# Expert rows gathered for two experts at once, gates moved to the addition of outputs, one eviction ahead of a branch, six probability buffers

## The chip, the cores and the metric

The kernel runs on 1 of the 8 cores of one Trainium2 chip. The metric is the device time of one execution in microseconds. Below, PE is TensorE, DVE is VectorE, ACT is ScalarE, POOL is GpSimd and SP is SyncE, whose queue issues the weight loads.

## The reference, cut to what matters

Twelve stages run on 256 tokens of width 1024 in float32. In order: a gated mixer, a dense feed-forward block, a second mixer, a **mixture of experts**, a dense block, an **attention stage "ab"** (16 heads of 64), a memory attention (4 heads of 256), two dense blocks, an **attention stage "c"** (16 heads with a neighbourhood bias), a memory attention, a dense block. The parts that the change touches:

```python
def moe_swiglu(x, w_router, e_gate, e_up, e_down):        # 8 experts, d_ff 3584
    logits = (t @ w_router).astype(jnp.float32)
    top_val, top_idx = lax.top_k(logits, TOP_K)           # TOP_K = 2
    top_w = jax.nn.softmax(top_val, axis=-1)
    gates = jnp.sum(jax.nn.one_hot(top_idx, N_EXPERTS) * top_w[..., None], axis=1)
    for e in range(N_EXPERTS):
        out = out + gates[:, e:e + 1] * swiglu(t, e_gate[e], e_up[e], e_down[e])
# attention, per head: p = softmax(q k^T * scale + bias) ; o = p v
```

## The kernel before, in words

**Engines and order.** Every engine has its program written out by hand, and engines meet at semaphores. A step such as `("xe", e, half)` is a count on the semaphore of the engine that makes it. The whole program is unrolled; the one branch is described below.

**Weights.** A ring of nine 2 MB slots is filled by SP. In the expert stage each slot is used as two halves of 1 MB, 18 in all, and a load waits until PE has released its half ("used"). In the other stages ACT copies each block to a rounded high part (L525) and DVE subtracts to get the low part (L533). PE then makes three products (L558 to L560).

**Experts.** The tokens of an expert are gathered into 96 slots, `expert_in` ("xe"). For each expert, `pe_gather` multiplies the 256 token rows (`copied`, the stationary operand, 128x128 blocks) by a 0/1 matrix `pick` (96 columns): 8 blocks of width times 2 blocks of tokens, 16 matmul calls, each of which is two records in the trace because the operands are float32. Then 4 more calls (8 records, 1 column each) gather the expert's gates for its slots into bank 7, and DVE copies them to `slot_gate`. The hidden width of 3584 is worked in 7 chunks (`NQ`) of 512. Chunk q of expert e, with c its number in the expert, runs on PE as: `pe_pair_up` (L1081), at c = 1 the scatter of the expert before, `pe_pair_down` of the chunk before (L1128), `pe_four_up` (L1095), `pe_four_down` (L1149), a transpose `pe_expert_turn` (L1113), at c = 1 a transpose of `pick`, and at c = 4 `pe_gather` of the next expert (L1057, then the gates, L1067). ACT applies silu and DVE multiplies silu, gate and up-projection (L2121, L2128). The scatter multiplies the output by `pick` transposed, and DVE adds the result to the token rows (L2089).

**Router and branch.** Before the experts, `dve_router` ranks the logits, gives each token its slot, makes `pick` for expert 0, then the gates, then a flag that says whether some expert has more than 96 tokens. `experts_again` lets PE gather for expert 0 and then makes every engine wait for the flag, load it to a register (L2444) and branch (L136). The body of the branch, a second pass over 16 half-experts, isn't run for these inputs. After the branch ACT evicts the gathered rows of expert 0 (`act_expert_rows`) and PE starts `pe_pair_up(0)`.

**Attention.** The 16 heads go in pairs. For pair j, PE makes the scores (L877), DVE adds the bias and takes the maximum (L1862), ACT takes the exponential (L1356), DVE normalizes (L1877), PE transposes (L890), ACT evicts the transpose (L1366) and PE weighs the values (L906). A head's probabilities lie in one of 4 buffers, so DVE's bias step of head i waits until head i-4 is transposed. PE's order in turn j is scores of pair j+1, weighing of pair j-2, transposes of pair j-1. DVE's order is bias of pair j, normalizing of pair j-1, low part of the output of pair j-3. In "c", POOL prepares each head's bias (L2287, L2289), and DVE subtracts the low parts of eight weight blocks (numbers 4 to 11) before its first bias step.

Of the kernel before, what the change touches and what calls it, by code (L numbers as in the profile page):

```python
# [5 lines left out]
P = 128  # L6
# [36 lines left out]
IN_ORDER = slice(PAIR, PAIR + SLOTS)  # L43
# [7 lines left out]
PAIRS = [(i, i + 1) for i in range(0, C_HEADS, 2)]  # L51
SINGLES = [(i,) for i in range(MEM_HEADS)]
# [5 lines left out]
def build_constants():  # L58
# [27 lines left out]
    low, high = np.arange(PAIR), np.arange(PAIR, SLOTS)  # L86
    add("slot_number", np.tile(np.concatenate([low, low, high, high, high, high]), (P, 1)))
# [51 lines left out]
class Program:  # L139
# [33 lines left out]
    def place_memory(self):  # L173
# [31 lines left out]
        self.slot_gate = put("slot_gate", [P, 2, 2])  # L205
# [27 lines left out]
        at[0] += 4096  # L233
# [8 lines left out]
        self.pick = over("pick", [P, TT, 2 * P], F32, small_at)  # L242
# [6 lines left out]
        def overlay(items):  # L249
# [33 lines left out]
            ("p3", [P, TT, T], F32, None),  # L283
# [6 lines left out]
            ("p3", [P, TT, T], F32, None), ("pT0", [P, TT, T], F32, None), ("pT1", [P, TT, T], F32, None),  # L290
# [6 lines left out]
        self.bank = [nc.alloc_psum_tensor(f"bank{i}", [P, 512], F32) for i in range(8)]  # L297

# [583 lines left out]
def pe_turn_p(p, st, prob, item):  # L882
    pe, nc = p.pe, p.nc
    for i in item:
# [3 lines left out]
        for qt in range(TT):  # L888
            for kt in range(TT):
                mm = nc.tensor.transpose(p.bank[6 + i % 2][:, kt * T + qt * P:kt * T + (qt + 1) * P],  # L890
                                         prob[i % 4][:, qt, kt * P:(kt + 1) * P], p.const("identity"))
# [46 lines left out]
def pe_ab(p, st):  # L938
# [27 lines left out]
    pe_attention(p, st, ab_heads(p, st), PAIRS, [g[f"p{i}"] for i in range(4)], [g["pT0"], g["pT1"]],  # L966
# [5 lines left out]
def pe_c(p, st):  # L972
# [23 lines left out]
    pe_attention(p, st, c_heads(p, st), PAIRS, [g[f"p{i}"] for i in range(4)], [g["pT0"], g["pT1"]], meanwhile)  # L996
# [3 lines left out]
def pe_mem(p, st):  # L1000
# [16 lines left out]
    pe_attention(p, st, mem_heads(p, st), SINGLES, [g[f"p{i}"] for i in range(4)], [g["pT0"], g["pT1"]], meanwhile)  # L1017
# [30 lines left out]
def pe_gather(p, e, new_gates=False):  # L1048
# [1533 lines left out]
```

## Time and profile before

| what | value |
|---|---|
| median of 3 runs | 2691.82 us (2688.63 to 2692.26) |
| profiled execution | 2692.51 us |
| its span, first to last instruction | 2691.3 us |
| PE busy | 2575.4 us (96%) |
| DVE, ACT, POOL busy | 1056.7, 817.7, 176.1 us |
| mean granted PE clock | 0.981 |
| read from HBM | 637.68 MB, 237 GB/s over the span |

The profile is of one execution. Ends of matmuls are modelled, so the distance between starts is what counts for PE. Idle time is put down to what ended it.

### The profile page before, as it was taken

To read this page: it belongs to the slowest core of one execution; us is meant where nothing else is said; L and a number is where in the kernel's file an instruction comes from. 1 tells how busy PE (TensorE), PEld (TensorE's weight loads), DVE (VectorE), ACT (ScalarE), POOL (GpSimd) and SP (SyncE) were. 2 spreads that over 40 slices of the span, in tenths; PEclk is the share of its full clock that TensorE was granted. 3 is DMA by queue.
4 is the path that set the end of the run, shared out by engine and by line. 5 is a ranking of instruction groups with operands and counts; after the bars stand their busy time and mean duration, and the time that the engine had idled before them with its cause. 6 is when DMAs were issued, how large, how long until landed. Compare 5 with 4: busy or idle time off the path is not lost.

```text
span 2691.3 us, 37633 instructions
## 1 busy us (share of the span) xinstructions
PE 2575.4 (96%) x16619; PEld 1747.7 (65%) x16619; DVE 1056.7 (39%) x1458; ACT 817.7 (30%) x1127; POOL 176.1 (7%) x178
## 2 busy tenths in 40 slices
PE   7999998999999999999998998899999998899998
PEld 5788776444444444444447886787887887688886
DVE  4655553010101011010106457736456444655544
ACT  4343342010101001010114435544344433544432
POOL 1200120000000000000000002000000004500000
PEclk9999998999999999999998999999999999899999
DMA  7555447999999999999985544345546547254651
GB/s 246 176 188 188 138 168 290 359 346 368 374 363 374 364 376 363 374 351 362 374 301 172 179 137 141 123 159 202 189 156 204 180 163 201 82 193 152 218 179 57
DMA packets 336507, 641.27 MB, mean 238 GB/s; under 512 B 16084, under 2 KB 128768, under 8 KB 336336
## 3 DMA queue, kind: packets, MB, share of 16 engines
q1 hardware_dynamic: 329840, 618.59, 64.7%
q0 software_dynamic: 6496, 20.20, 2.6%
q8 instruction: 132, 2.16, 0.3%
q14 instruction: 39, 0.32, 0.0%
HBM read 637.68 MB, written 1.05 MB: 237 GB/s over the span
## 4 chain that ended last, share of the span: by engine, by line
PE 89%; DVE 5%; ACT 2%; POOL 2%; DMA 1%; issue 1%; SPq 0%; ACTq 0%; DVEq 0%
PE bank L558 16%; PE bank L559 16%; PE bank L560 16%; PE bank L1081 15%; PE bank L1095 7%; PE bank L1128 7%; PE bank L1149 4%; DVE part_lo L533 2%; PE bank L877 1%; PE bank L1113 1%; PE bank L906 1%; PE bank L1057 1%; PE bank L729 1%; PE bank L570 1%; POOL bias L2153 1%; DMA raw<-in_w_in_dram 1%
## 5 line engine op out<-in xcount | busy, mean ns | idle before, releaser
L533 DVE TENSOR_TENSOR part_lo<-raw,part_hi 128x2048 fp32r<-128x2048 f32 x251 | 576.9, 2305 | 298.7 <-ACT part_hi L525 298.2
L525 ACT ACTIVATE part_hi<-raw 128x2048 fp32r<-128x2048 f32 x251 | 477.3, 1911 | 37.0 <-DMA raw<-in_c_w_in_dram 19.5
L558 PE MATMUL bank<-part_hi,x_hi 128*128 128x512 f32 x1088 | 445.3, 409 | 17.9 <-DVE part_lo L533 14.2
L559 PE MATMUL bank<-part_lo,x_hi 128*128 128x512 f32 x1088 | 438.3, 403 | 0.0
L560 PE MATMUL bank<-part_hi,x_lo 128*128 128x512 f32 x1088 | 432.0, 397 | 0.0
L558 PEld LDWEIGHTS bank<-part_hi,x_hi 128*128 128x128 f32 x1088 | 207.4, 191 | 67.4 <-DVE part_lo L533 20.5
L560 PEld LDWEIGHTS bank<-part_hi,x_lo 128*128 128x128 f32 x1088 | 207.4, 191 | 50.7
L559 PEld LDWEIGHTS bank<-part_lo,x_hi 128*128 128x128 f32 x1088 | 208.0, 191 | 43.8
L1081 PE MATMUL bank<-raw,expert_in 128*64 128x512 f32 x896 | 215.8, 603 | 2.5 <-ACT expert_in L1214 2.5
L1081 PE MATMUL bank<-raw_hi,expert_in 128*64 128x512 f32 x896 | 212.2, 594 | 0.0
L2121 DVE SCALAR_TENSOR_TENSOR h<-silu,slot_gate,bank 128x256 f32<-128x256 f32 x56 | 26.9, 480 | 462.3 <-ACT silu L1565 462.3
L558 PE MATMUL bank<-part_hi,hT_hi 128*128 128x512 f32 x440 | 173.6, 395 | 1.2 <-DVE hT_lo L1599 0.9
L559 PE MATMUL bank<-part_lo,hT_hi 128*128 128x512 f32 x440 | 173.3, 394 | 0.0
L560 PE MATMUL bank<-part_hi,hT_lo 128*128 128x512 f32 x440 | 171.9, 391 | 0.0
L1214 ACT ACTIVATE hT_hi<-bank 128x256 fp32r<-128x256 f32 x110 | 42.1, 383 | 399.0 <-PE bank L729 399.0
L2128 DVE SCALAR_TENSOR_TENSOR h<-silu,slot_gate,bank 128x128 f32<-128x128 f32 x56 | 19.4, 347 | 333.0 <-ACT silu L1571 333.0
L1081 PEld LDWEIGHTS bank<-raw_hi,expert_in 128*64 128x64 f32 x896 | 64.8, 138 | 129.2 <-issue 129.2
L1565 ACT ACTIVATE silu<-bank 128x256 f32<-128x256 f32 x56 | 21.5, 383 | 363.8 <-PE bank L1081 363.8
L1081 PEld LDWEIGHTS bank<-raw,expert_in 128*64 128x64 f32 x896 | 59.7, 137 | 107.4 <-issue 104.7
L1571 ACT ACTIVATE silu<-bank 128x128 f32<-128x128 f32 x56 | 15.5, 277 | 359.6 <-PE bank L1095 359.6
L1599 DVE TENSOR_TENSOR hT_lo<-bank,hT_hi 128x256 fp32r<-128x256 f32 x110 | 46.7, 424 | 196.5 <-ACT hT_hi L1214 196.5
L1095 PE MATMUL bank<-raw,expert_in 128*32 128x256 f32 x1792 | 118.6, 382 | 0.0
(268 smaller groups left out, 3476.4 us busy)
## 6 DMA issues: line engine op xcount, KB each, us to landing
raw<-in_exp_w_gate_dram SPq DMA_DIRECT2D x112, 512.0 KB, 6.6
raw<-in_exp_w_up_dram SPq DMA_DIRECT2D x112, 512.0 KB, 7.5
raw_hi<-in_exp_w_gate_dram SPq DMA_DIRECT2D x112, 512.0 KB, 8.4
raw_hi<-in_exp_w_up_dram SPq DMA_DIRECT2D x112, 512.0 KB, 9.2
raw<-in_exp_w_down_dram SPq DMA_DIRECT2D x56, 1024.0 KB, 12.8
raw_hi<-in_exp_w_down_dram SPq DMA_DIRECT2D x56, 1024.0 KB, 14.1
raw<-in_ffn_w_gate_dram SPq DMA_DIRECT2D x110, 512.0 KB, 4.0
raw<-in_ffn_w_up_dram SPq DMA_DIRECT2D x110, 512.0 KB, 5.2
```

What stands on the lines that cost most here:

```text
L525: p.nc.scalar.activation(p.part_hi[i][:, :], p.raw[i][:, :], ACT.Copy).then_inc(*self.rounded.step((name,)))
L533: p.nc.vector.tensor_tensor(p.part_lo[i][:, :], p.raw[i][:, :], p.part_hi[i][:, :].bitcast(F32), ALU.subtract).then_inc(*self.split.step(( ...
L558: nc.tensor.matmul(out, stat_hi, move_hi, start=start, stop=False, skip_group_check=True)
L559: nc.tensor.matmul(out, stat_hi, move_lo, start=False, stop=False, skip_group_check=True)
L560: return nc.tensor.matmul(out, stat_lo, move_hi, start=False, stop=stop, skip_group_check=True)
L570: mm = nc.tensor.transpose(p.bank[bank][:, k * P:(k + 1) * P], src[:, k * P:(k + 1) * P], p.const("identity"))
L1081: mm = p.nc.tensor.matmul(p.bank[4][half * PAIR:(half + 1) * PAIR, :].rearrange("p (m n) -> p m n", m=2), xe[:, kk, 0:PAIR], w[:, k, :, ha ...
L1095: mm = p.nc.tensor.matmul(p.bank[5][f * FOUR:(f + 1) * FOUR, 0:256].rearrange("p (m n) -> p m n", m=2), xe[:, kk, PAIR:SLOTS], w[:, k, :, ...
L1128: mm = p.nc.tensor.matmul(p.bank[0][half * PAIR:(half + 1) * PAIR, :], p.hT[:, j, d * PAIR:(d + 1) * PAIR], w[:, j, half * 512:(half + 1) ...
L1149: mm = p.nc.tensor.matmul(p.bank[1][f * FOUR:(f + 1) * FOUR, 0:256], p.hT[:, 2, tile * FOUR:(tile + 1) * FOUR], w[:, j, f * 256:(f + 1) * ...
L1214: p.nc.scalar.activation(dst, src, ACT.Copy).then_inc(*p.s.step(key))
L1599: p.nc.vector.tensor_tensor(dst, src, high.bitcast(F32), ALU.subtract).then_inc(*p.v.step(key))
```

## The change

Four edits. (1) Gates are no longer gathered into slots: the 4 one-column matmul calls, the `slot_gate` copy and the waits on both are gone, the hidden product becomes a plain multiplication, and the addition of an expert's output multiplies by the gate of the token row. (2) Experts 1 and 2, 3 and 4, 5 and 6 are gathered together: the same 16 calls with 192 columns, eight of them after chunk 4 and eight after chunk 5 of experts 0, 2 and 4. Expert 7 is gathered alone at chunk 4 of expert 6. There are three `expert_in` buffers for two, and two `pick` buffers of 96 columns for one of 256. (3) The flag is computed before the gates, and ACT evicts expert 0's rows ahead of the branch. (4) Six probability buffers for four; in "c" the low parts of blocks 10 and 11 are made after the first bias step. The constant `slot_number` shrinks from 256 to 96 columns.

```diff
-IN_ORDER = slice(PAIR, PAIR + SLOTS)
+PROB = 6
...
-def pe_gather(p, e, new_gates=False):
+def pe_gather(p, e):
...
-                mm = nc.tensor.matmul(out, p.copied[:, tt, k * P:(k + 1) * P], p.pick[:, tt, IN_ORDER],
+                mm = nc.tensor.matmul(out, p.copied[:, tt, k * P:(k + 1) * P], p.pick(e, tt),
...
-    if new_gates:
-        pe.wait_ge(*p.v.at("gates"))
-    if e:
-        pe.wait_ge(*p.s.at("pickT", e - 1))
-    for j in range(2):
-        for tt in range(TT):
-            mm = nc.tensor.matmul(p.bank[7][:, j:j + 1], p.pick[:, tt, j * P:(j + 1) * P], p.gates[:, tt, e % N_EXP:e % N_EXP + 1],
-                                  start=(j == 0 and tt == 0), stop=(tt == TT - 1), skip_group_check=True)
-    mm.then_inc(*p.t.step(("gate_gathered", e)))
+def gathered_in(e, count):
+    return [i for i in (e + 1, e + 2) if i < count] if e % 2 == 0 else []
...
+def pe_gather_two(p, group, part):
+    pe, nc = p.pe, p.nc
+    first, second = group
+    pe.wait_ge(*p.v.at("pick", second))
+    if part:
+        pe.wait_ge(*p.s.at("xe", second, 0))
+    elif first >= 2:
+        pe.wait_ge(*p.v.at("added", first - 2, 1, 1))
+    for n in range(4):
+        k = part * 4 + n
+        out = p.bank[2 + n // 2][:, (n % 2) * 2 * SLOTS:(n % 2 + 1) * 2 * SLOTS].rearrange("p (i s) -> p i s", i=2)
+        for tt in range(TT):
+            mm = nc.tensor.matmul(out, p.copied[:, tt, k * P:(k + 1) * P], p.picks[:, :, tt * SLOTS:(tt + 1) * SLOTS],
+                                  start=(n % 2 == 0 and tt == 0), stop=(tt == TT - 1), skip_group_check=True)
+    mm.then_inc(*p.t.step(("gathered", first, part)))
...
-        if c == 4 and e + 1 < count:
-            pe_gather(p, e + 1)
+        group = gathered_in(e, count)
+        if c in (4, 5) and len(group) == 2:
+            pe_gather_two(p, group, c - 4)
+        elif c == 4 and group:
+            pe_gather(p, *group)
...
+    p.act.wait_ge(*p.t.at("gathered", group[0], part))        # act_expert_rows, two experts
+    for i, e in enumerate(group):
+        for b in range(2):
+            at = part * 4 + 2 * b
+            made = p.nc.scalar.activation(
+                p.xe[e % 3][:, at:at + 2, :],
+                p.bank[2 + b][:, 0:4 * SLOTS].rearrange("p (k i s) -> p k i s", k=2, i=2)[:, :, i, :], ACT.Copy)
+        made.then_inc(*p.s.step(("xe", e, part)))
...
-            if i >= 4:
-                dve.wait_ge(*p.t.at("p_turned", st, i - 4))
+            if i >= PROB:
+                dve.wait_ge(*p.t.at("p_turned", st, i - PROB))
...
-    p.ring.subtract(*slots[4:12])
+    p.ring.subtract(*slots[4:10])
...
+                  {0: lambda: p.ring.subtract(slots[10], slots[11]), 1: lambda: p.ring.subtract(slots[12]), 3: lambda: p.ring.subtract(slots[13]),
...
-                nc.vector.tensor_tensor(part, part, p.bank[SCATTER_BANK[tt, half]][:, :], ALU.add).then_inc(
-                    *p.v.step(("added", e, half, tt)))
+                nc.vector.scalar_tensor_tensor(out=part, in0=p.bank[SCATTER_BANK[tt, half]][:, :],
+                                               scalar=p.gates[:, tt, e % N_EXP:e % N_EXP + 1], in1=part,
+                                               op0=ALU.mult, op1=ALU.add).then_inc(*p.v.step(("added", e, half, tt)))
...
-        nc.vector.scalar_tensor_tensor(out=p.h[0][:, :], in0=p.silu[0][:, :], scalar=gate[:, 0:1], in1=p.bank[4][:, 256:512],
-                                       op0=ALU.mult, op1=ALU.mult).then_inc(*p.v.step(("pair_h", q)))
+        nc.vector.tensor_tensor(p.h[0][:, :], p.silu[0][:, :], p.bank[4][:, 256:512], ALU.mult).then_inc(
+            *p.v.step(("pair_h", q)))
...
-    pe_gather(p, 0, new_gates=True)
+    pe_gather(p, 0)
+    act_expert_rows(p, [0], 0)
     for q in queues:
         q.wait_ge(*p.v.at("flag"))
```

## Rows read from the trace of the kernel before

**Rows 1.** The page's head: span, and PE's busy time, share and instructions.

```profile
span 2691.3 us, 37633 instructions
...
PE 2575.4 (96%) x16619; PEld 1747.7 (65%) x16619; DVE 1056.7 (39%) x1458; ACT 817.7 (30%) x1127; POOL 176.1 (7%) x178
```

**Rows 2.** Critical chain at chunk 4 of expert 0: start us, us, what.

```profile
530.53 3.55 PE bank L1057 x32
534.08 0.81 PE bank L1067 x8
```

**Rows 3.** Windows: one expert's turn and 10 us of it; busy by engine, PEclk, DMA, GB/s.

```profile
530.53:651.04 120.51, 120.51 (x1082) 52.80 (x1081) 11.79 (x26) 11.67 (x29) 0.00 (x0) 1.00 0.98 366
...
480.00:490.00 10.00, 10.00 (x68) 3.76 (x59) 0.57 (x2) 1.14 (x3) 0.00 (x0) 1.00 1.05 393
```

**Rows 4.** Waits of SP's queue, 450 to 1405 us: total, times, longest.

```profile
SPq L514 <- PE bank L1095: 616.0, 76, 17.4
```

**Rows 5.** Critical chain: matmuls of 128 and of 256 columns, 128x128 weights.

```profile
79.17 2.68 PE bank L808 x24
...
1789.99 3.69 PE bank L877 x16
```

**Rows 6.** Groups by form on DVE: busy, mean ns of one, idle before.

```profile
L1624 DVE SCALAR_TENSOR_TENSOR x_rows<-x_rows,bank 128x512 f32<-128x512 f32 x44 | 28.5, 681 | 21.4 <-PE bank L560 21.4
...
L2089 DVE TENSOR_TENSOR x_rows<-x_rows,bank 128x512 f32<-128x512 f32 x32 | 20.6, 682 | 2.1 <-PE bank L1184 1.5
```

**Rows 7.** PE's own queue: the flag's load and the branch, duration ns and start.

```profile
L2444 PEldq TENSOR_LOAD <-overflow x1: 490/490/490, 446.1 to 446.1; - x1
```

**Rows 8.** The same for the branch instruction of DVE and PE.

```profile
L136 DVEq COMPARE_BRANCH  x1: 72/72/72, 444.0 to 444.0; - x1
L136 PEldq COMPARE_BRANCH  x1: 3825/3825/3825, 446.7 to 446.7; - x1
```

**Rows 9.** Timeline around the branch, PE and ACT.

```profile
441.60 4.62 PE L1057 MATMUL bank<-pick,copied_rows 128*128 128x96 f32 x22 [1.01 <-DVE router_logits L2040]
```

**Rows 10.** The same, after the flag.

```profile
445.84 1.50 PE L1057 MATMUL bank<-pick,copied_rows 128*128 128x96 f32 x12
447.18 0.98 PE L1067 MATMUL bank<-gates,pick 128*128 128x1 f32 x8
...
449.62 0.87 ACT L1214 ACTIVATE expert_in<-bank 128x384 f32<-128x384 f32 x2
...
450.65 3.68 PE L1081 MATMUL bank<-raw,expert_in 128*64 128x512 f32 x8 [2.50 <-ACT expert_in L1214]
```

**Rows 11.** Stage ab, DVE's waits for transposes in all, 1640 to 1720 us.

```profile
DVE p L1862 <- PE bank L890: 5.6, 4, 2.0
```

**Rows 12.** Stage ab, timeline of ACT: two transposed query tiles evicted in turn 2.

```profile
1678.46 0.68 ACT L1214 ACTIVATE qT<-bank 128x256 f32<-128x256 f32 x2
```

**Rows 13.** Stage ab, PE: scores of pairs 4 and 5.

```profile
1678.94 1.13 PE L877 MATMUL bank<-kT,qT 64*128 64x256 f32 x8 [0.88 <-DVE softmax_stats L1874]
...
1683.69 1.13 PE L877 MATMUL bank<-kT,qT 64*128 64x256 f32 x8 [1.13 <-DVE softmax_stats L1874]
```

**Rows 14.** Stage ab, DVE: first bias step of pairs 4 and 6.

```profile
1681.83 0.48 DVE L1862 CUSTOM_DVE_ANT_0 p<-bank,consts,minus_sink 128x256 f32<-128x256 f32 x1 [1.25 <-PE bank L890]
...
1692.17 0.48 DVE L1862 CUSTOM_DVE_ANT_0 p<-bank,consts,minus_sink 128x256 f32<-128x256 f32 x1 [0.85 <-PE bank L890]
```

**Rows 15.** Stage c, timeline: POOL, DVE's subtractions 10 and 11, first bias step.

```profile
2285.17 3.09 POOL L2287 TENSOR_SCALAR bias<-bias 128x384 f32<-128x384 f32 x1
2287.16 5.59 DVE L533 TENSOR_TENSOR part_lo<-raw,part_hi 128x2048 fp32r<-128x2048 f32 x2
...
2292.66 0.41 DVE L1862 CUSTOM_DVE_ANT_1 p<-bank,bias 128x256 f32<-128x256 f32 x1
```

**Rows 16.** Stage c, PE: scores of pairs 0 and 1.

```profile
2285.46 2.08 PE L877 MATMUL bank<-kT,qT 64*128 64x256 f32 x8 [3.17 <-ACT kT L1214]
2294.26 2.08 PE L877 MATMUL bank<-kT,qT 64*128 64x256 f32 x8 [6.73 <-DVE softmax_stats L1862]
```

More of the change, by code:

```diff
@@ L85, in build_constants @@
     add("scan_keep", np.tile((np.arange(2 * T) % GLA_CHUNK != 0).astype(np.float32), (P, 1)))
-    low, high = np.arange(PAIR), np.arange(PAIR, SLOTS)
-    add("slot_number", np.tile(np.concatenate([low, low, high, high, high, high]), (P, 1)))
+    add("slot_number", np.tile(np.arange(SLOTS), (P, 1)))
     e = np.arange(N_EXP)
@@ L232, in place_memory @@
         y0_at = at[0]
-        at[0] += 4096
+        at[0] += 8192
         end = at[0]
@@ L297, in place_memory, with prob, pick @@
         self.bank = [nc.alloc_psum_tensor(f"bank{i}", [P, 512], F32) for i in range(8)]
+    def prob(self, tensors):
+        return [tensors[f"p{i}"] for i in range(PROB)]
+    def pick(self, e, tt):
+        return self.picks[:, (e - 1) % 2, tt * SLOTS:(tt + 1) * SLOTS]
     def const(self, name):
@@ L1352, in act_attention @@
         for i in items[j] if j < m else ():
-            hd, P_ = heads[i], prob[i % 4]
+            hd, P_ = heads[i], prob[i % PROB]
             act.wait_ge(*p.v.at("biased", st, i))
@@ L1522, in act_router, with act_expert_rows @@
         nc.scalar.activation(x, x, ACT.Copy, scale=alpha).then_inc(*p.s.step(("total", n)))
-def act_expert_rows(p, e):
-    if e >= 2:
-        p.act.wait_ge(*p.t.at("four_up", (e - 1) * NQ - 1))
-    for half in range(2):
-        p.act.wait_ge(*p.t.at("gathered", e, half))
-        act_high_and(p, p.xe[e % 2][:, half * 4:half * 4 + 4, :],
-                     p.bank[2 + half][:, 0:4 * SLOTS].rearrange("p (k s) -> p k s", k=4), "xe", e, half)
+def act_expert_rows(p, group, part, into=None):
+    for e in group:
+        if e >= 3:
+            p.act.wait_ge(*p.t.at("four_up", (e - 2) * NQ - 1))
+    if len(group) == 1:
+        for half in range(2):
+            p.act.wait_ge(*p.t.at("gathered", *group, half))
+            act_high_and(p, p.xe[group[0] % 3 if into is None else into][:, half * 4:half * 4 + 4, :],
+                         p.bank[2 + half][:, 0:4 * SLOTS].rearrange("p (k s) -> p k s", k=4), "xe", *group, half)
+        return
+    p.act.wait_ge(*p.t.at("gathered", group[0], part))
[6 more added lines that the diff above has]
+        made.then_inc(*p.s.step(("xe", e, part)))
 def act_experts(p, st, count, ahead=None):
@@ L1584, in act_experts @@
             act_high_and(p, p.pickT[0:SLOTS, :, :], p.bank[7][0:SLOTS, 0:TT * P].rearrange("p (t s) -> p t s", t=TT), "pickT", e)
-        if c == 4 and e + 1 < count:
-            act_expert_rows(p, e + 1)
+        group = gathered_in(e, count)
+        if c == 4 and group or c == 5 and len(group) == 2:
+            act_expert_rows(p, group, c - 4)
     if ahead is not None:
@@ L1862, in dve_attention @@
                 made = nc.vector.tensor_tensor_reduce(
-                    out=rows(prob[i % 4][:, qt, :]), in0=rows(p.bank[4 + i % 2][:, qt * T:(qt + 1) * T]), in1=bias,
+                    out=rows(prob[i % PROB][:, qt, :]), in0=rows(p.bank[4 + i % 2][:, qt * T:(qt + 1) * T]), in1=bias,
                     scale=-scale, scalar=3e38 if hd["sink"] is None else hd["minus_sink"], op0=ALU.add, op1=ALU.min,
@@ L2037, in dve_router @@
     dve_pick(p, 0, 0)
+    nc.vector.tensor_reduce(p.biggest[:, :], out[:, 2 * E:3 * E], AX.X, ALU.max).then_inc(*p.v.step(("biggest",)))
+    dve.wait_ge(*p.v.at("biggest"))
+    nc.vector.tensor_scalar(p.overflow[:, :], p.biggest[:, :], float(SLOTS), None, ALU.is_gt).then_inc(*p.v.step(("flag",)))
     dve.wait_ge(*p.s.at("second_weight"))
@@ L2082, in add @@
             dve.wait_ge(*p.s.at("total", 3))
+            dve.wait_ge(*p.v.at("gates"))
         for tt in halves:
@@ L2127, in dve_experts @@
         dve.wait_ge(*p.s.at("four_silu", q))
-        nc.vector.scalar_tensor_tensor(out=p.h[1][:, 0:P], in0=p.silu[1][:, 0:P], scalar=gate[:, 1:2], in1=p.bank[5][:, P:2 * P],
-                                       op0=ALU.mult, op1=ALU.mult).then_inc(*p.v.step(("four_h", q)))
+        nc.vector.tensor_tensor(p.h[1][:, 0:P], p.silu[1][:, 0:P], p.bank[5][:, P:2 * P], ALU.mult).then_inc(
+            *p.v.step(("four_h", q)))
         if c == 0 and e:
@@ L2132, in dve_experts @@
             y_low(e - 1)
-        if e + 1 < count:
-            if c == 2:
-                dve_pick(p, e + 1, first)
-            if c == 4:
-                dve_slot_gate(p, e + 1)
+        for coming in gathered_in(e, count) if c == 2 else ():
+            dve_pick(p, coming, first)
     if ahead is not None:
```

75 lines of the change are left out of this document (34 added, 41 removed).

## Prediction

> **What bounds the kernel now.** I read the page first: of a span of 2691.3 us PE is busy for 2575.4 [rows 1], so a part counts only if it shortens PE's work or one of PE's waits. I then took the windows and the critical chain through the expert stage. One expert's turn is 120.51 us long with PE busy throughout at a granted clock of 1.00 [rows 3], and the chain there is PE alone, one block behind the other. At chunk 4 it shows the gather as a piece of its own, 3.55 us for 32 records, and the gate gather behind it, 0.81 us for 8 [rows 2]. The DMA share of 0.98 in the same row could make one think of a stage bound by its loads. Two rows speak against it: SP's queue spent 616 us of the stage waiting for PE to free a slot [rows 4], and where loads are outstanding the engines move 393 GB/s against a mean of 366 [rows 3]. So loads follow PE, with 7% to spare. Last I read the timelines around the branch and of both attention stages, where PE does stand idle.
>
> **Part 1 and 2, gathers.** Seven gathers stand in the stage behind the branch (experts 1 to 7). Each costs 3.55 + 0.81 = 4.36 us [rows 2], 30.5 in all. The seven gate gathers (5.7 us) go away altogether. What is left is three gathers for two experts and one for expert 7 alone (3.55). The price of a record with 192 columns isn't in the trace. A record of 1, 96 or 128 columns takes 0.81 / 8 = 0.10, 3.55 / 32 = 0.111 and 2.68 / 24 = 0.112 us [rows 2, 5]: up to 128 columns it costs the same, so something other than the columns sets it, and the 128x128 weights that each record loads are what these have in common. A record of 256 columns takes 3.69 / 16 = 0.231 [rows 5], so there the columns do. In proportion 192 columns take 0.173; allowing a little for a fixed part in it I take 0.17, thus 5.4 us for two experts. The new sum is 3 x 5.4 + 3.55 = 19.8, a **saving of 10.8 us**. The bounds are the two neighbouring prices: 0.111 gives 14.2 in all and a saving of 16.3, 0.231 gives 25.7 and a saving of 4.8.
>
> A rule of the Trainium skill speaks for a cheaper record. "TensorE: Matmul & The Clock Gate", section "Back-to-back issue gap", gives N / 2.4 + 2.5 ns at full clock, 82.5 ns for 192 columns, which is less than the weights' price in [rows 2]; by it the record would stay at 0.111. But it gives 109 ns for 256 columns where [rows 5] show 231, so for these float32 records the trace does not agree, and my sum goes by the row.
>
> Work that goes with it is hidden. DVE's product loses its gate and its addition gains one. A DVE addition of 128x512 from a bank takes 682 ns, and a multiply-and-add of that shape 681 [rows 6]; the gate as a per-row factor I price at the same (a dearer one is covered: DVE is busy for 11.8 of 120.5 us [rows 3], and PE has two blocks to do before it needs the additions). ACT makes eight evictions of 128x192 in place of four of 128x384, under PE's next chunk; it too is busy for 11.7 us. If that cover were gone, the eviction (0.9 us for two of the old ones [rows 10]) would be paid once for each of three groups. The second half of a joint gather waits for the eviction of the first, a whole chunk behind it; PE's later work is queued behind that wait, but it is met some ten us early. The scatter's wait for "xe" is now for a gather of an earlier expert or chunk. SP's loads are moved past nothing; their spacing only shrinks by 1%: 366 GB/s become 366 x 120.5 / 119.1 = 370, against the 393 seen.
>
> **Part 3, the branch.** PE's first product after it starts at 450.65 [rows 10]. ACT's eviction ends at 450.5, but PE's own branch instruction starts at 446.7 and takes 3.83 us [rows 8], so it ends at 450.5 too: moving the eviction ahead removes one of two equal waits. What moves the other is the queue. PE's load of the flag starts at 446.1 [rows 7], when records up to 448.2 are still to run: some nine of the gather and eight of the gates, 17 in the queue. Without the gates' eight, the load is reached eight records earlier. These run at 4.62 / 22 = 0.21 us [rows 9] or, late, at 0.11, so 0.9 to 1.7 us earlier; I take 1.2. PE then leaves its branch at about 449.3, the eviction ends at about 447.9, and ACT's own branch, priced as PE's (0.5 for the flag's load and 3.8), by 452.3. PE's first block gives it work only later: 8 of its 32 records take 3.68 us [rows 10], the other 24 at least half as much each, so the block lasts over 8 us. The flag no longer waits for the gates; nothing waited for it. **1.2 us**, from 0 (a fetch that takes longer because weight loads are still running) to 2.5.
>
> **Part 4, six buffers, stage ab.** DVE waits 5.6 us for transposes, in four waits [rows 11]. All four go, but PE must gain from it. The scores of pair 4 start at 1678.94, directly behind ACT's query tile of 1678.46 + 0.39 [rows 12, 13]: the first two waits are given back there. From pair 5 on PE waits for the bias step: 1.13 us idle before 1683.69 [rows 13], released by DVE, whose steps of pairs 4 and 6 had waited 1.25 and 0.85 [rows 14]. I add these two and a little for the slack they free: **2.3 us**, bounds 0 and 5.6. The memory stages have four heads and never reuse a buffer; nothing there.
>
> **Part 4, stage c.** The first bias step starts at 2292.66, behind the subtractions of blocks 10 and 11, 5.59 us from 2287.16 [rows 15]. PE's scores of pair 0 are done at 2285.46 + 2.08 = 2287.54 [rows 16], so the step can run at 2287.6. PE's scores of pair 1 start 1.6 us behind the step's start (2292.66 to 2294.26), thus at about 2289.2 in place of 2294.26: 5.1 us less idle time of the 6.73 [rows 16]. The two subtractions move behind it; they are late for nobody, since PE reads block 10 only after pair 2's scores. POOL's bias of head 3 is then next in line. POOL and DVE slow each other there (3.09 us for a step [rows 15]), but PE has 36 products queued between the scores of pair 1 and pair 2. Behind that PE is bound by its own work, so I keep the gain. The transposes waited for in c are PE's own order; the two extra buffers bring nothing that I can name. **5.1 us**, from 0 (POOL late) to 7 (also less time at half clock: both scores take 2.08 us for eight records, against 1.13 at the full clock [rows 13]).
>
> **Constants.** 160 columns less are 82 KB ahead of the first weights, at 393 GB/s **0.2 us**.
>
> **The sum** is 10.8 + 1.2 + 2.3 + 5.1 + 0.2 = 19.6. The span becomes 2671.7. The profiled execution took 1.2 us more than its span, and the median shown is 0.7 below it: 2672.2 us. (What cannot be told from no change here is about 0.2%, 5.4 us.)
>
> **The rivals.** (a) *Weights still set the record of 192 columns.* For it: 1 to 128 columns cost the same. Against it: 256 columns cost double. Saving 16.3 in place of 10.8: **2666.7**. This is where the Trainium skill's rule above would lead. Chance 0.12. (b) *The columns cost more, as 256 do.* The moving operand is now in two pieces, 192 floats apart. **2678.2**, chance 0.07. (c) *Stage c gives its gain back*: POOL's bias or a block's landing becomes the wait. For it: one of POOL's two steps for a head takes 3.09 us while DVE subtracts [rows 15]. Against it: PE's 36 products. **2677.3**, chance 0.10. (d) *The attention edits do nothing at all*, PE's idle time only moves: 2672.2 + 7.4 = **2679.6**, chance 0.05. (e) *Loads become the bound*, the slower case. Place: the expert stage, once PE asks for 370 GB/s. If the mean delivered stays at the 366 of now, the 10.8 us are lost, 2683, still faster; it decides against the change when the rate falls below 366: at 355 GB/s an expert takes 124.2 us and the stage 8 x 3.7 = 30 us more, less the 8.8 of the other parts: **2713**. Nothing that lowers the rate is in the diff, and SP waits for PE for 616 us. Chance 0.02 for slower, 0.02 for the 2683 case. The forecast itself has the rest, 0.62.
>
> **How the numbers follow.** The low end takes in (a) with the shorter half-clock stretch, 2666.7 - 1.9, about 2665. The high end takes in (b), (c) and (d), 2680. Together they leave out (e), two of the slow cases at once, and noise of the runs (3.6 us between the three shown), some 0.15. Faster by over 0.2% means below 2686.4: all but (e) and a surprise, 0.96; within 0.2% 0.02; slower 0.02.
>
> **What would show it.** The L1067 group is gone, and the joint gather stands as two pieces of 16 records with 2.7 us each at chunks 4 and 5 of experts 0, 2 and 4; 1.8 says (a), 3.7 says (b). Two turns of experts, a joint gather in one of them, take some 237.7 us in place of 241.0. PE leaves the branch near 449.3. DVE in ab has no wait on L890, and PE starts the output projection 2.3 us sooner after its first scores. In c the gap before the scores of pair 1 is 1.6 us. It is wrong if PE shows new waits for "xe", for a landing, or for POOL's bias, or if the granted clock falls in other places than now.

## The result and the profile after

The changed kernel takes 2661.28 us (median of four runs, 2658.41 to 2662.33) against 2692.04: a ratio of 0.989, with a 95% interval of 0.9877 to 0.9903. It is 30.8 us faster where 19.6 were forecast, and below the forecast's low end of 2665. The profiled execution is the fastest of the four; its span is 2657.2 us. From the head of its page, to be read beside [rows 1]:

```profile
span 2657.2 us, 37338 instructions
...
PE 2553.2 (96%) x16459; PEld 1730.9 (65%) x16459; DVE 1047.0 (39%) x1450; ACT 817.1 (31%) x1138; POOL 178.0 (7%) x178
```

PE is busy for 22.2 us less, and stands idle for 11.9 less.

The critical chain around the branch (start us, us, what). L1065 is the single gather, L1108 the first block of pair 0:

```profile
438.03 6.67 PE bank L1065 x32
444.73 0.50 ACT expert_in L1243
445.23 0.27 issue
445.49 7.09 PE bank L1108 x32
```

the same block in the kernel before:

```profile
450.65 9.69 PE bank L1081 x32
```

and PE's own branch, in the view of that line (duration ns, start us), to be read beside [rows 8]:

```profile
L135 PEldq COMPARE_BRANCH  x1: 3665/3665/3665, 441.7 to 441.7; - x1
```

The eviction ends at 445.2 and PE's branch at 441.7 + 3.67 = 445.3. As in the kernel before, two waits end together. They end sooner, and the block behind them is shorter. Windows of just that block (columns as in [rows 3]) show why, before and after: a granted clock of 0.73 and of 1.00, so in the kernel before a part of it ran at 1.2 GHz.

```profile
450.65:460.34 9.69, 9.69 (x36) 3.13 (x40) 0.00 (x0) 1.14 (x1) 0.00 (x0) 0.73 0.01 2
...
445.49:452.58 7.09, 7.09 (x36) 2.70 (x40) 0.00 (x0) 1.28 (x1) 0.00 (x0) 1.00 0.02 5
```

The chain at the joint gathers behind experts 0 and 2 (L1094), to be read beside [rows 2]:

```profile
522.71 2.60 PE bank L1094 x16
525.31 7.02 PE bank L1108 x32
...
541.55 2.60 PE bank L1094 x16
...
760.18 2.60 PE bank L1094 x16
```

Sixteen records of 192 columns take 2.60 us, 0.163 us each. Two experts' turns take 760.18 - 522.71 = 237.47 us, against twice the 120.51 of [rows 3]. The waits of SP's queue are 605 us for PE's L1122 (the block that [rows 4] have as L1095), so loads still follow PE.

Stage ab as two windows of the same extent, from one POOL step to the same one in the next stage (us, then busy us of PE, PEld, DVE, ACT, POOL, then PEclk, DMA share, GB/s), first the kernel before:

```profile
1610.94:1730.50 119.56, 98.48 (x524) 75.65 (x524) 85.57 (x208) 65.53 (x140) 16.55 (x17) 0.96 0.31 107
```

and the changed one:

```profile
1590.75:1707.54 116.79, 99.65 (x524) 76.12 (x524) 85.52 (x208) 64.97 (x140) 16.53 (x16) 0.94 0.32 109
```

PE's idle time, the window less its busy time, is 17.1 us in place of 21.1. DVE's 5.6 us of waits for transposes [rows 11] are gone from its list.

Stage c, timeline of PE's scores of pairs 0 and 1, to be read beside [rows 16]:

```profile
2258.24 1.14 PE L885 MATMUL bank<-kT,qT 64*128 64x256 f32 x8 [2.22 <-ACT kT L1243]
2261.29 2.08 PE L885 MATMUL bank<-kT,qT 64*128 64x256 f32 x8 [1.91 <-DVE softmax_stats L1902]
```

The gap before the scores of pair 1 is 1.91 us in place of 6.73.

So each part of the change can be seen, near its forecast size or above it, and yet 11 us more are gained. Most of that lies elsewhere. A stage whose instructions are the same in both kernels shows it: the eighth stage, dense, from POOL's step for the first half of the rows to the same step of the next stage. Timeline of POOL, before:

```profile
2028.57 0.56 POOL L2183 TENSOR_TENSOR rstd<-rstd,minus_half 128x1 f32<-128x1 f32 x1 [172.42 <-DVE rstd L1636]
...
2221.79 0.56 POOL L2183 TENSOR_TENSOR rstd<-rstd,minus_half 128x1 f32<-128x1 f32 x1 [172.41 <-DVE rstd L1636]
```

and after:

```profile
2004.75 0.56 POOL L2214 TENSOR_TENSOR rstd<-rstd,minus_half 128x1 f32<-128x1 f32 x1 [171.76 <-DVE rstd L1676]
...
2197.30 0.56 POOL L2214 TENSOR_TENSOR rstd<-rstd,minus_half 128x1 f32<-128x1 f32 x1 [171.76 <-DVE rstd L1676]
```

193.22 us before, 192.55 after, with nothing edited in between. The groups of the lines view (busy us, mean ns of one, idle before) say which records it is, before:

```profile
L558 PE MATMUL bank<-part_hi,x_hi 128*128 128x512 f32 x1088 | 445.3, 409 | 17.9 <-DVE part_lo L533 14.2 <-DVE x_lo L1599 3.7
L559 PE MATMUL bank<-part_lo,x_hi 128*128 128x512 f32 x1088 | 438.3, 403 | 0.0
L560 PE MATMUL bank<-part_hi,x_lo 128*128 128x512 f32 x1088 | 432.0, 397 | 0.0
```

and after:

```profile
L566 PE MATMUL bank<-part_hi,x_hi 128*128 128x512 f32 x1088 | 444.2, 408 | 19.1 <-DVE part_lo L541 15.4 <-DVE x_lo L1639 3.7
L567 PE MATMUL bank<-part_lo,x_hi 128*128 128x512 f32 x1088 | 433.5, 398 | 0.0
L568 PE MATMUL bank<-part_hi,x_lo 128*128 128x512 f32 x1088 | 432.8, 398 | 0.0
```

The middle product of each group of three (the low part of the weights by the high part of the tokens) takes 398 ns in place of 403. These two tables give modelled lengths. Taken from start to start over all 512-column records of a product at the full clock (those with the tokens, and those of the down-projections and output projections), the three are 231.5, 234.4 and 230.3 ns apart before, and 231.2, 231.7 and 231.4 after.

### The profile page after: what moved, and what is told of

Same layout as the page of the kernel before. It is cut to its first block, busy times and chain, and to the rows that moved or that the text cites. A ratio compares the mean times of both kernels' runs of the same rounds, so it can differ in the third digit from the quotient of the medians.

```text
span 2657.2 us, 37338 instructions
## 1 busy us (share of the span) xinstructions
PE 2553.2 (96%) x16459; PEld 1730.9 (65%) x16459; DVE 1047.0 (39%) x1450; ACT 817.1 (31%) x1138; POOL 178.0 (7%) x178
## 4 chain that ended last, share of the span: by engine, by line
PE 89%; DVE 5%; ACT 3%; DMA 2%; issue 1%; POOL 0%; SPq 0%; DVEq 0%
PE bank L566 16%; PE bank L567 16%; PE bank L568 16%; PE bank L1108 15%; PE bank L1122 8%; PE bank L1155 7%; PE bank L1176 4%; DVE part_lo L541 2%; PE bank L885 1%; PE bank L1140 1%; ACT part_hi L533 1%; PE bank L737 1%; PE bank L578 1%; DMA raw<-in_c_w_in_dram 1%; PE bank L914 1%; DMA raw<-in_w_in_dram 1%
## 5 line engine op out<-in xcount | busy, mean ns | idle before, releaser
L2155 DVE TENSOR_TENSOR h<-silu,bank 128x256 f32<-128x256 f32 x56 | 23.6, 421 | 497.2 <-ACT silu L1604 497.2
L1108 PE MATMUL bank<-raw,expert_in 128*64 128x512 f32 x896 | 214.1, 598 | 0.8 <-ACT expert_in L1243 0.8
L1108 PE MATMUL bank<-raw_hi,expert_in 128*64 128x512 f32 x896 | 211.3, 592 | 0.0
L2162 DVE TENSOR_TENSOR h<-silu,bank 128x128 f32<-128x128 f32 x56 | 16.1, 288 | 334.2 <-ACT silu L1610 334.2
L1108 PEld LDWEIGHTS bank<-raw_hi,expert_in 128*64 128x64 f32 x896 | 64.5, 137 | 127.7 <-issue 127.7
L1108 PEld LDWEIGHTS bank<-raw,expert_in 128*64 128x64 f32 x896 | 59.5, 136 | 106.4 <-issue 105.3
L1610 ACT ACTIVATE silu<-bank 128x128 f32<-128x128 f32 x56 | 15.5, 278 | 359.4 <-PE bank L1122 359.4
L1122 PE MATMUL bank<-raw,expert_in 128*32 128x256 f32 x1792 | 118.6, 382 | 0.0
```

Of the source, the lines that this page charges most:

```text
L1108: mm = p.nc.tensor.matmul(p.bank[4][half * PAIR:(half + 1) * PAIR, :].rearrange("p (m n) -> p m n", m=2), xe[:, kk, 0:PAIR], w[:, k, :, ha ...
L1122: mm = p.nc.tensor.matmul(p.bank[5][f * FOUR:(f + 1) * FOUR, 0:256].rearrange("p (m n) -> p m n", m=2), xe[:, kk, PAIR:SLOTS], w[:, k, :, ...
```

## The experiments

"Experts" below is the stretch from POOL's last normalising step ahead of the router to its first behind the experts; "ab" and "c" are the stretches between two such steps around these attentions (c from POOL's first bias step on). "Distance" is the address of the first weight buffer less that of `x_hi`, the token parts, modulo 256 bytes; all weight buffers are 16384 bytes apart and so share it. The table holds all kernels; readings follow one by one.

| kernel | distance | stage 8, us | experts | ab | c | median us | ratio to before, 95% interval |
|---|---|---|---|---|---|---|---|
| before | 96 | 193.22 | 993.4 | 119.6 | 95.7 | 2692.0 | |
| changed | 192 | 192.55 | 977.1 | 116.8 | 89.9 | 2661.3 | 0.9890 (0.9877-0.9903) |
| again | 192 | 192.55 | 977.4 | 121.5 | 89.9 | 2663.95 | 0.9896 (0.9881-0.9911) |
| c_order_back | 192 | 192.5 | 977.5 | 119.6 | 94.1 | 2667.0 | 0.9906 (0.9893-0.9920) |
| four_probs | 192 | 192.6 | 977.6 | 119.8 | 90.4 | 2665.2 | 0.9903 (0.9888-0.9919) |
| same_places | 96 | 193.25 | 979.3 | 119.2 | 91.6 | 2670.3 | 0.9920 (0.9906-0.9933) |
| one_by_one | 192 | 192.6 | 984.4 | 119.6 | 93.1 | 2672.5 | 0.9933 (0.9919-0.9947) |
| branch_back | 192 | 192.6 | 980.9 | 119.7 | 89.9 | 2667.9 | 0.9919 (0.9905-0.9932) |
| before_moved | 192 | 192.55 | 991.7 | 119.9 | 97.8 | 2681.95 | 0.9969 (0.9957-0.9981) |
| moved_320 | 0 | 189.35 | 976.6 | 119.1 | 89.4 | 2647.0 | 0.9840 (0.9827-0.9854) |
| before_32 | 128 | 191.78 | 992.4 | 121.0 | 95.8 | 2675.5 | 0.9948 (0.9935-0.9962) |
| moved_64 | 0 | 189.35 | 979.0 | 118.1 | 90.8 | 2642.4 | 0.9826 (0.9811-0.9841) |
| moved_96 | 32 | 191.78 | 977.3 | 120.0 | 90.1 | 2659.8 | 0.9885 (0.9870-0.9900) |
| moved_448 | 128 | 191.68 | 979.2 | 118.3 | 90.3 | 2653.1 | 0.9860 (0.9845-0.9875) |
| x_apart | 128 | 191.51 | 979.1 | 119.7 | 90.9 | 2657.9 | 0.9876 (0.9861-0.9892) |
| x_with_0 | 0 | 191.12 | 979.1 | 121.0 | 90.5 | 2640.8 | 0.9816 (0.9803-0.9830) |
| x_with_64 | 0 | 189.67 | 977.0 | 119.3 | 89.4 | 2647.9 | 0.9840 (0.9827-0.9854) |
| before_160 | 0 | 189.32 | 993.3 | 119.4 | 94.9 | 2667.25 | 0.9917 (0.9904-0.9931) |

**again**: the changed kernel, no edit.

> The changed kernel itself, once more, to see what one profile of it differs from the next. Theory A (what the first profile gained before the router, 3.4 us in stages whose instructions are the same, comes from where the buffers lie): the same 3.4 us within 0.5, the same spacing of the dense stages' 512-column records (231.6, 232.3, 231.9 ns against 232.2, 235.7, 230.6 before), the same rows of the granted clock at half. Rival B (it was a lucky execution): the gain before the router anywhere between 0 and 3.4 us, and the records' spacing changes from one profile to the next.

Stage 8 and the records repeat to 0.03 us and 0.1 ns. The gain ahead of the router is 1.6 us, not 3.4: here PE was granted half the clock for 3.4 us more near the start. Theory A holds for the records; of the 3.4 us, some 1.8 belong to that one execution. The stages that can be read to a few hundredths are those in which PE never stands still, at full clock. The median is 2663.95, 2.7 us above that of the first comparison, so a difference of some 3 us between two comparisons shows nothing.

**c_order_back**: the subtractions of stage c in their old order.

```
-    p.ring.subtract(*slots[4:10])
+    p.ring.subtract(*slots[4:12])
...
-                  {0: lambda: p.ring.subtract(slots[10], slots[11]), 1: lambda: p.ring.subtract(slots[12]), ...
+                  {1: lambda: p.ring.subtract(slots[12]), ...
```

> The changed kernel with the subtractions of stage c in their old order (all eight weight blocks ahead of the first bias step). The prediction's step: the time of it is lost again, 5.1 us of 2661.3, so 2666.4, and PE stands still 6 to 7 us before the scores of pair 1 instead of 1.9. Rival 1: the biases landed 3 us earlier in the changed kernel's profile and the subtractions now fit before them; then it costs under 2 us. Rival 2: all that stage c gained (8.8 us) hangs on the order, by the subtractions that POOL slowed down: 2670.

Its timeline of PE has

```profile
2262.34 1.32 PE L885 MATMUL bank<-kT,qT 64*128 64x256 f32 x8 [2.77 <-ACT kT L1243]
2271.08 2.08 PE L885 MATMUL bank<-kT,qT 64*128 64x256 f32 x8 [7.43 <-DVE softmax_stats L1902]
```

The gap is back, 7.43 us against 1.91. c takes 94.1 us against 89.9, 4.2 more, and the median rises by 3.1. The step is confirmed, with 4.2 us by the stage and 5.5 by the gap; both rivals fall.

**four_probs**: four buffers used, six kept in memory.

```
-PROB = 6
+PROB = 4
```

> The changed kernel with four probability buffers used instead of six, all buffers where they are. The prediction's step: 2.3 us lost, all of it in stage ab (first bias step of a pair waiting for a turned block of probabilities again), none in stage c and the memory stages: 2663.6. Rival 1: buffers are free in time either way, under 0.5 us. Rival 2: they also carry stage c, where PE would then wait again before the scores of later pairs: 2666 to 2669.

DVE's list of waits in ab has the transposes again:

```profile
DVE p L1902 <- PE bank L898: 6.0, 4, 2.0
```

and the window of the stage reads

```profile
1593.00:1712.80 119.80, 99.76 (x524) 76.55 (x524) 85.44 (x208) 65.55 (x140) 16.55 (x16) 0.94 0.30 106
```

Idle time of PE is 20.0 us again. So the mechanism is right: two buffers more take 3 us of idle time from PE. But `again`, with six buffers, shows what becomes of them:

```profile
1592.82:1714.34 121.52, 104.29 (x524) 79.55 (x524) 85.66 (x208) 65.31 (x140) 16.55 (x17) 0.90 0.30 105
```

It idles for 17.2 us and is busy for 104.3, since its granted clock in the stage is 0.90. Over all the profiles, the five kernels with four buffers (before, before_32, before_moved, before_160, four_probs) idle for 20.0 to 21.2 us in ab and take 119.4 to 121.0, mean 119.9; the thirteen with six idle for 16.9 to 18.4 and take 116.8 to 121.5, mean 119.4. The idle time goes and the stage hardly gets shorter: PE works the same products at a lower mean clock. The clock's own records say so too: in ab PE was granted half the clock for 10.2 to 13.7 us with four buffers (mean 13.0) and for 13.7 to 23.9 with six (mean 18.9). The medians differ by 1.3 us, within the spread. In c four buffers cost 0.5 us. The gain of this part is near 0.5 us, less than the spread of these stages, and not 2.3; that the clock takes the rest back is read from these rows and not tested by itself.

**same_places**: all buffers behind the constants at their old addresses.

```
+        at[0] += 640
         self.params = put("param_rows", [P, P])
...
+        at[0] += 32
         self.overflow = put("overflow", [P, 1], mybir.dt.int32)
```

> The changed kernel with 640 bytes left free behind the constants and 32 behind the routing marks, so that the weight buffers and all behind them lie at the addresses of the kernel before (the change makes the constants 160 columns shorter and drops a small tile). Theory A (placement): the 512-column records of the dense stages go back to a mean of 232.9 ns from 231.9, each of the five dense stages after the first loses 0.66 us, and the stages before the router lose their 3.4 us: 2661.3 + 3.3 + up to 3.4 = 2664.6 to 2668. Rival B (chance, or the change's other parts): within 1 us of the changed kernel, with the records as there.

Stage 8 takes 193.25 us, as in the kernel before; the records are 231.5, 234.4 and 230.5 ns apart, as there:

```profile
L569 PE MATMUL bank<-part_lo,x_hi 128*128 128x512 f32 x1088 | 438.2, 403 | 0.0
```

The median rises by 6.35 us. Theory A holds. Shorter constants (640 bytes) and the dropped `slot_gate` (32) move every weight buffer by 672 bytes, and that alone is worth 6 us of the result. Against the kernel before (2692.31 in this comparison) the change with its places held is worth 22.0 us. Its first block behind the branch is not at the full clock:

```profile
449.72 8.73 PE bank L1110 x32
```

**one_by_one**: a joint record issued as two single ones.

```
+            for i in range(2):
-            mm = nc.tensor.matmul(out, p.copied[:, tt, k * P:(k + 1) * P], p.picks[:, :, tt * SLOTS:(tt + 1) * SLOTS],
+                mm = nc.tensor.matmul(out[:, i, :], p.copied[:, tt, k * P:(k + 1) * P], p.picks[:, i, ...],
```

> The changed kernel with each joint gather record of 192 columns issued as two records of 96, same banks, same places in the program: 96 more records. The prediction's step (a record of 192 columns 0.163 us against 0.111 for one of 96): the two cost 0.222 us, 0.059 us more per pair, 96 pairs: 5.7 us lost, in the three pairs of pieces (16 joint records took 2.60 us; 32 single ones should take 3.55). Rival (the 128-partition weight load isn't what sets a 96-column record and the second record of the same weights is cheaper): under 2 us lost.

Its chain has the pieces at the old price:

```profile
524.55 3.55 PE bank L1095 x32
```

3.55 us against 2.60, six times: 5.7 us, as forecast. The stretch takes 7.0 more; another 1.0 is the first block behind the branch, 8.1 us against 7.09. The granted clock of that block is 1.00 here, so it isn't the clock; what lengthens it is open. The median is 8.6 above that of `again`; the profile has 3.2 us more in stage c too, where nothing was edited.

**branch_back**: first eviction behind the branch, flag behind the gates.

```
     pe_gather(p, 0)
-    act_expert_rows(p, [0], 0)
     for q in queues:
...
+    act_expert_rows(p, [0], 0)
     act_experts(p, moe, N_EXP, lambda: act_ahead(p, moe + 1, 0, 1))
```

(and the two instructions of the flag moved to the end of the router's function).

> The changed kernel with the first eviction behind the branch again and the flag worked out behind the gates. The prediction's step: the branch stretch loses 1.2 to 1.7 us (ACT waits for the flag, takes its branch, loads its table and only then evicts, 1.28 and 0.98 us behind TensorE's own branch of 3.67 us), and the first pair_up stands behind it. Rival 1: TensorE's own branch ends last either way, under 0.5 us. Rival 2: the longer stand of TensorE also brings the granted clock down for the first pair_up (9.69 us before, 7.09 after): 3.5 to 4.5 us lost.

Timeline of ACT and PE behind the branch:

```profile
446.19 1.28 ACT L1243 ACT_TABLE_LOAD   x1 [5.90 <-issue]
447.48 0.87 ACT L1243 ACTIVATE expert_in<-bank 128x384 f32<-128x384 f32 x2
```

```profile
448.03 3.63 PE L1108 MATMUL bank<-raw,expert_in 128*64 128x512 f32 x8 [2.70 <-ACT expert_in L1243]
```

ACT is past its branch instruction (45 ns, at 441.0) but issues nothing until 446.2, then loads its table and evicts; PE's branch is over at 446.0, and PE waits until 448.03. The first block takes 8.78 us and not 7.09, at a granted clock of 0.81. Experts lose 3.5 us, the figure of rival 2: 1.7 for the later start and 1.7 for the clock.

The two halves are not equally sure. From POOL's step ahead of the router to the start of this block it takes 22.4 to 22.7 us in all thirteen kernels with the early eviction, and 24.0 to 24.5 in the five without (branch_back and the four made from the kernel before). The block itself takes 8.7 to 9.8 us in those five. With the early eviction it takes 7.1 in seven kernels, but 8.1 in one_by_one and 8.7 or 8.8 in five (same_places, moved_64, moved_448, x_apart, x_with_0), each of which has a stretch at half clock over it. So the 1.7 us of waiting are shown; the clock's share comes and goes with the execution and can't be put down to the edit by one run. In the mean of these profiles it is some 1.3 us.

**before_moved**: the kernel before, weight buffers moved by 1376 bytes.

```
+        at[0] += 1376
         self.params = put("param_rows", [P, P])
```

> The kernel before with 1376 bytes left free behind the constants, nothing else: its weight buffers then lie 2048 bytes beyond those of the changed kernel. Theory A (placement, by the address modulo a power of two up to 2048): the middle product's 512-column records fall from 234.4 to 231.7 ns and the kernel gains what same_places lost, 4 to 7 us: 2686 to 2688 of 2692.3. Theory A' (placement, but another condition): records of another spacing, any sign. Rival B (the records' spacing came with the shorter constants or the other parts of the change): 2692.3, records of 234.4 ns.

Records of 231.3, 231.7 and 231.4 ns, stage 8 in 192.55 us, the very figures of the changed kernel, in a program with no other edit. It gains 8.7 us. Theory A holds from the other side too.

**moved_320**: the changed kernel, 320 bytes at the same place (the edit of all kernels below is this line with another number, where no other is shown).

```
+        at[0] += 320
         self.params = put("param_rows", [P, P])
```

> The changed kernel with 320 bytes left free behind the constants, half of the way back to the old addresses. By theory A the spacing of the 512-column records is that of the one, that of the other or a third; if it goes in proportion to the shift it lies half-way: 2667. No number was had for it beforehand; it tells whether places can be chosen with profit.

Not between the two: records of 227.1, 227.5 and 228.1 ns, stage 8 in 189.35 us, and 2647.0. It is 17 us below `again`, by a change of no instruction.

**before_32, moved_64, moved_96, moved_448**: which addresses are the good ones?

> The kernel before with 32 bytes left free behind the constants, nothing else. The first weight buffer then begins at byte 62720 of a partition, a multiple of 128 (before: 62688, 96 past one; the changed kernel: 62016, 64 past one; moved_320: 62336, a multiple; before_moved: 64064, 64 past one). Theory C (what counts is whether the weight buffers begin at a multiple of 128 bytes, at 64 past one, or at an odd 32): the dense stages' 512-column records fall from 231.5, 234.4 and 230.3 ns to about 227.5 each, and the time from 2690.6 by what same_places and moved_320 differ, 23 us: 2667. Rival D (the address as a whole, or a larger power of two, counts): records of another spacing, a gain between 0 and 10 us.

> The changed kernel with 64 bytes left free behind the constants: weight buffers at 62080, a multiple of 128. Theory C: as moved_320, records of 227.5 ns, 2647. Rival D: near the changed kernel's 2664, or any other.

> The changed kernel with 96 bytes left free behind the constants: weight buffers at 62112, 32 past a multiple of 128. Theory C: as same_places (there 96 past one), records of 231.5, 234.4 and 230.3 ns, 2670; if 32 past and 96 past differ, a third set. Rival D: near the changed kernel's 2664.

> The changed kernel with 448 bytes left free behind the constants: weight buffers at 62464, a multiple of 1024 (moved_320's are multiples of 128 but not of 256). Theory C: 2647, as moved_320. Rival (a multiple of a larger power of two is better still): under 2644, records below 227 ns.

Theory C fails. moved_64 is fast as it says (2642.4), but before_32 and moved_448 have weights that begin at multiples of 256 (moved_448 at one of 1024 even), and records of 230.3 to 231.1 ns. moved_96 is not like same_places either. By the lines view, moved_64 has

```profile
L567 PE MATMUL bank<-part_hi,x_hi 128*128 128x512 f32 x1088 | 438.3, 403 | 18.8 <-DVE part_lo L542 15.1 <-DVE x_lo L1640 3.7
...
L569 PE MATMUL bank<-part_hi,x_lo 128*128 128x512 f32 x1088 | 428.3, 394 | 0.0
L568 PE MATMUL bank<-part_lo,x_hi 128*128 128x512 f32 x1088 | 427.7, 393 | 0.0
```

and moved_448

```profile
L567 PE MATMUL bank<-part_hi,x_hi 128*128 128x512 f32 x1088 | 444.6, 409 | 17.3 <-DVE part_lo L542 13.6 <-DVE x_lo L1640 3.8
L568 PE MATMUL bank<-part_lo,x_hi 128*128 128x512 f32 x1088 | 433.4, 398 | 0.0
```

Both fast kernels have their weights 128 bytes past a multiple of 256, and so do the token parts `x_hi` at 16512 in every kernel so far. Two theories were left: the distance between the two operands, or the weights' own address.

**x_apart, x_with_0, x_with_64**: the token parts moved as well.

```
+        at[0] += 128            # x_with_64: 192
         x_at = at[0]
...
+        at[0] += 128            # x_with_64: 64
         self.rows = put("x_rows", [P, TT, D])
...
+        at[0] += 64             # x_with_0: 192, x_with_64: none
         self.params = put("param_rows", [P, P])
```

> The changed kernel with the weight buffers where moved_320 has them (62336, 128 past a multiple of 256) and the token parts x_hi and x_lo, which begin at 16512 (also 128 past a multiple of 256) in all kernels so far, moved on by 128 bytes to 16640, a multiple of 256. Theory E (records are short where the weights' address and that of the token parts with which they are multiplied differ by a multiple of 256 bytes): no longer so, records of about 230.7 ns, 2653 to 2660. Theory F (only the weights' own address counts, 128 past a multiple of 256 being the good one): records of 227.5 ns, 2642 to 2647.

> The changed kernel with the weight buffers where moved_448 has them (62464, a multiple of 256) and the token parts at 16640, a multiple of 256 too. Theory E: the two agree, records of 227.5 ns, 2642 to 2647. Theory F: as moved_448, records of 230.3 to 231.0 ns, 2653.

> The changed kernel with the weight buffers 64 bytes past a multiple of 256, as they are in the changed kernel itself (here 62272), and the token parts at 16704, 64 past one as well. Theory E: records of 227.5 ns, 2642 to 2647. Theory F: as the changed kernel, records of 231.2 to 231.7 ns, 2664.

All three go by theory E. x_apart has the weights of a fast kernel and a distance of 128: records of 230.2 to 230.3 ns and 2657.9 us. x_with_0 and x_with_64 have the weights of slow ones and a distance of 0: 227.2 to 228.3 ns, 2640.8 and 2647.9. The lines view of x_with_0:

```profile
L569 PE MATMUL bank<-part_hi,x_hi 128*128 128x512 f32 x1088 | 439.7, 404 | 18.0 <-DVE part_lo L544 14.2 <-DVE x_lo L1642 3.7
L571 PE MATMUL bank<-part_hi,x_lo 128*128 128x512 f32 x1088 | 428.7, 394 | 0.0
L570 PE MATMUL bank<-part_lo,x_hi 128*128 128x512 f32 x1088 | 427.2, 393 | 0.0
```

Its stage 8 is long (191.12) for another reason: the window of that stage shows a granted clock of 0.99, where those of the other kernels are at 1.00 throughout.

**before_160**: the kernel before with a distance of 0.

> The kernel before with 160 bytes left free behind the constants: weight buffers at 62848, 128 past a multiple of 256, as the token parts are. Theory E and theory F: records of 227.5 ns in the dense stages, and against the changed kernel at such a place (moved_64 2642.4, moved_320 2647.0) what the change itself is worth with the places made equal: by the prediction's sum, less its 0.2 for the constants, 19.4 us, so 2662 to 2666; by the chip's sum so far (24.3 between before and same_places less what is chance) up to 22 us, so 2664 to 2669.

2667.25 us, 22 below the kernel before, by one line. Against moved_64 and moved_320 the change is worth 24.8 and 20.2 us; against x_with_0 and x_with_64, timed beside it, 26.4 and 19.4.

## Why the prediction was wrong

The step that failed is **Constants**. It priced 160 columns less by the bytes that need not be fetched, "82 KB ahead of the first weights, at 393 GB/s 0.2 us", and took the rest of the memory plan as without weight. The same edit, with the dropped `slot_gate`, moves nine weight buffers from a distance of 96 bytes to one of 192 from the tokens with which they are multiplied. That is worth 6.4 us (same_places) to 8.7 (before_moved), and the sum had no term for it. No bound was asked for it either, so the range's low end of 2665 was too high. Without it the change gives 22.0 us with the old places and 19.4 to 26.4 with good ones, where the forecast's other terms make 19.4.

Point by point, by its own terms:

- **Gathers, 10.8.** Six pieces of 2.60 and one single gather of 3.55 make 19.2 in place of 30.5: 11.4 saved. 0.163 us a record where 0.17 was taken. Rivals (a) with 1.8 us a piece and (b) with 3.7 fall. By the rule that the Trainium skill's "TensorE: Matmul & The Clock Gate", section "Back-to-back issue gap", gives for a matmul on its own, the columns would take 82.5 ns; for these records the trace, with 163, does not agree. Two turns took 237.47 us, forecast 237.7.
- **Branch, 1.2.** Right in its cause, too small. PE's product behind the branch starts 5.16 us sooner, 3.4 of which were there ahead of the router: 1.75. What was missing is the clock: the first block takes 7.09 us in place of 9.69. branch_back puts both at 3.5 us, of which 1.7 are the wait that the prediction meant. The rest is the clock's share, which five of the thirteen kernels with the edit did not get. The prediction had read the price of the half clock only in c.
- **Stage ab, 2.3.** The wait goes and 3 us of idle time with it (four_probs), but the stage gets shorter by some 0.5. It counted the idle time removed as time gained.
- **Stage c, 5.1.** The scores of pair 1 stood 6.73 us, now 1.91 (forecast 1.6). Putting the order back costs 4.2 in c. Rival (c) falls: no POOL or landing wait took its place. Rival (d), no effect of the attention edits, holds for ab alone. The stretch ahead of it was 1.7 us shorter in same_places and 3.0 in the first profile. In the latter POOL waited 12.5 us for the biases to land, and 15.5 before. But that stretch takes 57.4 us in the kernel before and 51.2 in before_32, which differs from it by 32 bytes, so I can't tell a gain of 1.7 there from its own spread; what sets the landing stays open.
- **Rival (e), loads.** Fell: SP waits for PE for 605 us.

That the parts make 11.4 + 3.5 + 0.5 + 4.2 = 19.6, the very sum that was forecast, is luck: the gathers and the branch gave 2.9 us more than their terms, the attention stages 2.7 less. With 6.4 for the places, 2.4 of the 28.4 us between `again` and the kernel before remain; the entry of c, 54.9 us in `again` against 57.4, may be that. The further 2.4 of the first comparison's 30.8 lie within what two comparisons of the same kernel differ by (2661.28 and 2663.95).

## What to carry to other kernels

An edit that changes the size of anything in a hand-laid memory plan moves all that is behind it; print the addresses of the large operands before and after, and when a stage without any edit changes its time, look there first. In a kernel bound by products in series, try the memory plan as a parameter: one line with 64 bytes took the changed kernel from 28.4 to 48.0 us below the kernel before (`again` and moved_64, each against its own comparison), more than any single part of the change was worth. And idle time of PE next to a stretch at half clock is not a gain in hand: count what the clock does with it, on either side.

## What the runs showed of the hardware

- **The time from the start of one record to the next goes by the distance modulo 256 bytes between the model's weights and the tokens.** In these products a 128x128 block of tokens is loaded into PE and 512 columns of weights stream past it. At the full clock, means over all records of 512 columns: 227.1 to 228.3 ns at a distance of 0 (five kernels, five pairs of addresses), 230.2 to 231.1 at 128 and 32, 231.2 to 231.7 at 192, and 231.5 / 234.4 / 230.3 for the three products at 96. Stage 8 in all of the kernels goes by the distance alone: 189.3 to 189.7 (x_with_0's aside), 191.5 to 191.8, 192.5 to 192.6, 193.2. For the records with tokens alone it is 227.2 to 229.2 at 0, 231.7 to 233.5 at 128 and 32, 233.0 to 233.7 at 192, and 232.8 to 232.9, 236.9 to 237.1 and 231.4 to 231.7 at 96. A record's own two operands are not the whole of it. In the down-projections the loaded block is `hT`, which lies a multiple of 256 bytes behind the weights in every kernel, and yet these records change too: 230.8, 232.0 and 229.1 ns before, 226.8 to 226.9 in moved_64. In the output projections the loaded block lies so too, and there the records don't change (226.9 to 228.2 in all kernels). The last `hT` record ahead of a record with tokens takes 236.7 before, 225.8 in the changed kernel, 232.5 in x_apart and 226.7 in moved_64, so the operand of the next record has a part in it. Which access collides with which is open; so are the distances not tried. The Trainium skill's page "SBUF — State Buffer", section "Operand start alignment", asks only that an operand start at a multiple of its element's size, which all these addresses do, and says that its runs timed nothing.
- It isn't so for every shape. The 256-column products of the mixers are, if anything, slower at a distance of 0 (medians of 120 ns against 118 at 192), and the expert blocks' records don't react (means of 216.5 to 216.6 ns for L1108's in all kernels but one_by_one, and 54.6 for L1122's in all).
- **A record's price between 128 and 256 columns** was open: 0.163 us for 192, against 0.112 and 0.231 [rows 5].
- **PE's branch** took 3.67 to 3.97 us in the eighteen profiles, and ACT, in branch_back, issued nothing for 5.1 us behind a branch instruction of its own of 45 ns.
